# Two layers of a hybrid decoder: causal masks as matrix products, small S5 operations on GpSimd, six early input units instead of four

## The chip, the cores and the metric

One core of a Trainium2 chip runs the kernel. The metric is device microseconds of one execution. All times below are microseconds (us) unless they are marked ns. The engines are TensorE (PE, its weight loads PEld), VectorE (DVE), ScalarE (ACT), GpSimd (POOL) and SyncE (SP, which here only issues transfers).

## What is computed

One step of a decoder of two layers, for a prompt of 256 tokens and 8 samples with one new token each. The model has 1024 columns. Each layer computes (the reference, cut):

```python
h = x @ p['w_in']                      # 1024 x 2560
u_a, q_b, k_b, v_b, q_c, k_c, v_c, g_c = jnp.split(h, ...)
ya, s5r, s5i = s5_branch(u_a, ...)     # complex diagonal state space model
yb = sb_attend(q_b, k_b, v_b, bias, ...)          # 4 heads of 64
yc, ret_s = retention_branch(q_c, k_c, v_c, g_c, ...)
x = layer_norm(ALPHA * x + concat(ya, yb, yc) @ p['w_out'])
f, conv_new = conv_ffn(x, conv_prev, w_up, conv_w, conv_b, w_down)
x = layer_norm(ALPHA * x + f)
```

and in stick_breaking, where the mask is:

```python
z = q @ k * DH ** -0.5 + bias
valid = k_pos[None, :] < q_pos[:, None]
log_beta = jax.nn.log_sigmoid(z)
log_rest = jnp.where(valid, log_beta - z, 0.0)
tail = lax.cumsum(log_rest, axis=3, reverse=True) - log_rest
w = jnp.where(valid, jnp.exp(log_beta + tail), 0.0)
```

The S5 branch has 16 groups of 64 complex states. The prompt's states come from a scan over 256 steps; a sample's new state is a * x0 + f * (B u), and the prompt's last state is scaled by f too. All data are f32.

## The kernel before

**Data.** x lies transposed, 128 partitions x 8 blocks x 264 columns (256 prompt, 8 samples). The weights of a layer are cut into 94 units of 8 blocks of 128x128 (512 KB), which SP loads into a ring of 5 slots: 20 input units, 8 of w_out, 44 up, 22 down. One unit gives one tile of 128 output columns.

**Two ways to multiply.** Of the input units, 0 to 2 are taken raw ahead of the layer norm, and the others are f32 products, eight a unit (`tile8`, L432). An f32 product leaves two records in the trace. Nearly all units behind the inputs, and the units in EARLY, are split: weight and x become a high half (fp32r, rounded) and the low rest, and the product is hi x hi, hi x lo and lo x hi in one pass each (L439 to L441; L451 to L453 for the early ones). EARLY[1] is 16 to 19 before. For an early unit ScalarE writes we_hi (`split_hi_early`, L972), VectorE subtracts it from the ring's slot in place (`split_lo_early`, L1586), and x is split once, by ScalarE's `upper_early` (L978, xe_hi) and VectorE's two `lower_early` (L1593, xe_lo, four blocks of x each). TensorE waits for a unit's low half before its first product. An early unit's slot in the ring is used like any other.

**Order.** The order on each engine is written out by hand; the engines meet only through semaphores (`need` waits for a count, `claim` waits until a PSUM bank is read out). A table says behind which input unit each side step stands. In layer 0: the scores of the attention (sc) behind unit 7, S5's inputs of the first half (`s5_b`, b00, b01) at 2 and 3, of the second half (b10, b11) at 9 and 11, S5's readout c0 at 11 and c1 at 17, the tails at 16. In layer 1: scores behind 5, b10 at 6, b11 and c0 at 7, tails and c1 at 12, the gated products (glu, L581), retention (L633) and key transposes at 14.

**Attention.** q and k are rows of hb, a head has 64 of the 128 partitions: heads 0 and 2 the lower, 1 and 3 the upper half. `causal` gives each head's scores in two products (L622: 256 columns, L623: the second 128x128 block), `sb_scores` calls it for the four heads. ScalarE evacuates them to ZT (Z in the code, L1145) and makes softplus; VectorE multiplies the diagonal 128x128 blocks by a 0/1 mask (`sb_second`, L1877 and L1878), TensorE sums the tails (`sb_tails`, L744 to L751), VectorE subtracts (`sb_third`, L1884 to L1889), ScalarE takes exp, and VectorE multiplies by the mask again (`sb_mask`, L1894 and L1895).

**S5.** `s5_b` gives the inputs (L554, four products of 32 rows side by side), ScalarE copies them to BR and BI (`s5_evac`, L1139), VectorE scans (L1746, L1747), turns back (`s5_post`, L1781 to L1787) and takes the last states sfin (L1789, L1790). cf (L1665 to L1671) are the readout's coefficients. `s5_c` is the readout: 16 records for the prompt (L566), 16 for the samples (L571), which come from VectorE's small operations `s5_states` (six of 128x32, L1719 to L1725) and `s5_samples` (eight of 128x32, L1756 to L1765) for each half. `s5_finals` (six of 128x8, L1769 to L1775) makes the prompt's last states. `s5_skip` (L1968) adds D u to the readout.

**ScalarE in layer 0** also makes the tables of S5's turns (`turns_up`, L1091 to L1093). L1251 (zs) copies the samples' scores behind the main ones' place.

## Time and profile before

| | before |
|---|---|
| median of 3 runs | 674.18 |
| lowest, highest | 674.04, 674.87 |
| profiled execution | 674.94 |
| its span | 673.1 |
| TensorE busy | 661.4 (98%) |
| VectorE busy | 569.1 (85%) |
| ScalarE busy | 415.2 (62%) |
| GpSimd busy | 91.2 (14%) |
| TensorE's granted clock | full in all of the 40 slices |

The span goes from the first to the last instruction; the profiled execution's own time is 1.84 us longer. Engines work at the same time, so their busy times don't add up to the span. An engine does its instructions in order: one that waits holds all behind it.

### The profile page before, as it was taken

How to read it: one execution, taken by the hardware profiler on the slowest of the kernel's cores; microseconds unless marked ns; L12 is line 12 of the kernel's file. 1: busy time of each engine (PE TensorE's matmuls, PEld its weight loads, DVE VectorE, ACT ScalarE, POOL GpSimd, SP SyncE). 2: the span in 40 equal slices, each digit the busy share in tenths (PEclk: the TensorE clock that was granted, in tenths of full speed). 3: DMA queues.
4: the chain of work that ended last, by engine and by line, in shares of the span. 5: the costliest groups of instructions: out<-in, count | busy, mean ns of one | idle time of the engine just before them, and what ended most of it. 6: DMA issues, size and time to landing. Idle time of an engine off the chain costs nothing. (4 is left out here: it accounts for less than half of the span.)

```text
span 673.1 us, 13390 instructions
## 1 busy us (share of the span) xinstructions
PE 661.4 (98%) x5024; PEld 613.4 (91%) x5024; DVE 569.1 (85%) x1195; ACT 415.2 (62%) x690; POOL 91.2 (14%) x90
## 2 busy tenths in 40 slices
PE   8999999999999999999999999999999999999997
PEld 6777887989999999999987787989999999999996
DVE  5999999989998988789588998898999898884653
ACT  5776348758676666655847536786867666663343
POOL 0000010150222222200200000106012222220001
PEclk9999999999999999999999999999999999999999
DMA  8777540746674655664456463354765556555411
GB/s 315 244 274 220 188 130 6 274 112 227 203 255 151 201 187 184 197 192 142 142 179 228 167 206 125 115 200 167 199 211 197 188 170 193 176 196 190 161 57 66
DMA packets 42915, 121.82 MB, mean 181 GB/s; under 512 B 5538, under 2 KB 15170, under 8 KB 42338
## 3 DMA queue, kind: packets, MB, share of 16 engines
q1 hardware_dynamic: 40466, 115.22, 51.7%
q0 software_dynamic: 1088, 4.11, 2.5%
q10 hardware_dynamic: 1296, 1.63, 0.8%
q8 instruction: 40, 0.66, 0.4%
q14 instruction: 25, 0.20, 0.1%
HBM read 115.33 MB, written 5.61 MB: 180 GB/s over the span
## 5 line engine op out<-in xcount | busy, mean ns | idle before, releaser
L1579 DVE TENSOR_TENSOR w_lo<-ring,w_hi 128x1024 fp32r<-128x1024 f32 x144 | 175.4, 1220 | 30.6 <-ACT w_hi L964 29.0
L439 PE MATMUL ps<-x_hi,w_hi 128*128 128x264 f32 x672 | 191.0, 284 | 1.0 <-DVE x_lo L1529 1.0
L440 PE MATMUL ps<-x_lo,w_hi 128*128 128x264 f32 x672 | 190.4, 283 | 0.0
L441 PE MATMUL ps<-x_hi,w_lo 128*128 128x264 f32 x672 | 190.3, 283 | 0.0
L964 ACT CAST w_hi<-ring 128x1024 fp32r<-128x1024 f32 x144 | 150.2, 1043 | 59.4 <-PE ps L441 58.7
L439 PEld LDWEIGHTS ps<-x_hi,w_hi 128*128 128x128 f32 x672 | 126.5, 188 | 1.9 <-issue 1.8
L440 PEld LDWEIGHTS ps<-x_lo,w_hi 128*128 128x128 f32 x672 | 126.6, 188 | 0.0
L441 PEld LDWEIGHTS ps<-x_hi,w_lo 128*128 128x128 f32 x672 | 126.0, 188 | 0.0
L432 PE MATMUL ps<-x,ring 128*128 128x264 f32 x480 | 112.1, 390 | 0.1
L432 PEld LDWEIGHTS ps<-x,ring 128*128 128x128 f32 x480 | 89.1, 190 | 18.9 <-issue 2.2
L439 PE MATMUL ps<-hff_hi,w_hi 128*128 128x264 f32 x352 | 100.0, 284 | 0.0
L441 PE MATMUL ps<-hff_hi,w_lo 128*128 128x264 f32 x352 | 99.9, 284 | 0.0
L440 PE MATMUL ps<-hff_lo,w_hi 128*128 128x264 f32 x352 | 99.9, 284 | 0.0
L2190 POOL TENSOR_TENSOR hff_lo<-conv,hff_hi 128x264 fp32r<-128x264 f32 x44 | 52.7, 1198 | 213.8 <-ACT hff_hi L1208 213.8
L441 PEld LDWEIGHTS ps<-hff_hi,w_lo 128*128 128x128 f32 x352 | 66.3, 188 | 0.0
L439 PEld LDWEIGHTS ps<-hff_hi,w_hi 128*128 128x128 f32 x352 | 66.1, 188 | 0.0
L440 PEld LDWEIGHTS ps<-hff_lo,w_hi 128*128 128x128 f32 x352 | 66.1, 188 | 0.0
L1365 ACT ACTIVATE conv<-ps,vec 128x264 f32<-128x264 f32 x84 | 47.8, 569 | 22.2 <-PE ps L441 22.1
L1208 ACT CAST hff_hi<-conv 128x264 fp32r<-128x264 f32 x44 | 18.2, 414 | 48.8 <-DVE conv L1600 48.8
L2117 DVE SCALAR_TENSOR_TENSOR conv<-ps,vec,conv 128x254 f32<-128x254 f32 x84 | 40.5, 482 | 3.0
L1223 ACT COPY hb<-ps 128x264 f32<-128x264 f32 x34 | 12.7, 374 | 46.0 <-PE ps L432 43.5
L503 PE MATMUL ps<-zg,ring 128*128 128x266 f32 x160 | 39.0, 388 | 1.6 <-DMA ring<-in_units 1.6
(364 smaller groups left out, 1091.0 us busy)
## 6 DMA issues: line engine op xcount, KB each, us to landing
ring<-in_units SPq DMA_DIRECT2D x187, 512.0 KB, 3.5
kv<-in_kpool SPq DMA_DIRECT2D x32, 128.0 KB, 2.4
kv<-in_vpool SPq DMA_DIRECT2D x32, 128.0 KB, 2.4
SR<-in_sret SPq DMA_DIRECT2D x2, 1024.0 KB, 5.9
out_rsample<-SR POOLq DMA_DIRECT2D x2, 1024.0 KB, 5.1
out_kv<-hb ACTq DMA_DIRECT2D x2, 528.0 KB, 4.4
VBC<-v_rows POOLq DMA_DIRECT2D x8, 128.0 KB, 3.5
out_y<-x SPq DMA_DIRECT2D x3, 264.0 KB, 2.1
```

Of the source, the lines that this page charges most:

```text
L432: ins = mm(out, ring[:, ring_slot(n), k], rhs(k), start=(k == 0), stop=(k == 7))
L439: mm(out, wh, hi, start=start, stop=False)
L440: mm(out, wh, lo, start=False, stop=False)
L441: return mm(out, wl, hi, start=False, stop=stop)
L503: ins = mm(out[:, 0:GB], ring[:, ring_slot(raw_unit(q, i)), k], zgs[q % 2][:, k], start=(k == 0), stop=(k == KT - 1))
L964: E.did(nc.scalar.copy(w_hi[:, split_slot(i)], ring[:, ring_slot(n)]), "w_hi")
L1208: E.did(nc.scalar.copy(hff_hi[:, p], conv[:, (2 * p + 1) % CSLOTS]), "hff_hi")
L1223: E.did(nc.scalar.copy(hb[:, i], ps[:, in_bank(i), 0:T]), "in_evac")
L1365: E.did(f(conv[:, i % CSLOTS], source, ACT.Identity, scale=pv(L, "cw2", i), bias=pv(L, "cb", i)), "fc")
L1579: E.did(tt(w_lo[:, slot], ring[:, ring_slot(L * UNITS + i)], w_hi[:, slot].bitcast(F32), ALU.subtract), "w_lo")
L2117: E.did(stt(c[:, 2:SEQ], bank[:, 0:SEQ - 2], pv(L, "cw0", i), c[:, 2:SEQ], ALU.mult, ALU.add), "up_free")
L2190: E.did(tt(hff_lo[:, p], conv[:, (2 * p + 1) % CSLOTS], hff_hi[:, p].bitcast(F32), ALU.subtract), "hff_lo")
```

## The change

1. EARLY[1] is 14 to 19. The six we_hi share four homes in work and turn; units 18 and 19 wait until their home is free. In layer 1 ScalarE casts unit 14 behind upper_early, unit 15 behind the copy of tile 13, and 16 to 19 at glu. VectorE does both lower_early and the low half of 14 ahead of rotary, and the low half of 15 behind it.
2. The constant mask (0 or 1) becomes unseen (0 or -2^30). Two fp32r copies, of the identity and of unseen, are made by ScalarE in layer 0 behind unit 7's work. `causal` has a third product for each head, one-pass, 128 rows, 256 columns, which adds unseen to both diagonal blocks in PSUM. `sb_scores` waits for the two copies. VectorE's four mask products of a layer are gone.
3. s5_states, s5_samples and s5_finals are done by GpSimd, in its order ahead of its first transfer of each layer. It waits for x0, cf, the copies of the inputs, and the last states. New waits for its count: TensorE ahead of the samples' readout (L571), ScalarE ahead of the copy of the second half's inputs, SP ahead of the next layer's parameters.

```diff
-EARLY = [[], [16, 17, 18, 19]]
+EARLY = [[], [14, 15, 16, 17, 18, 19]]
...
-                 for e, (home, plane) in enumerate((("work", 0), ("work", 1), ("turn", 0), ("work", 3)))]
+                 for e, (home, plane) in enumerate((("work", 0), ("work", 1), ("turn", 0), ("work", 2), ("work", 0), ("work", 3)))]
...
-                mm(bank[:, 0:SEQ], kk[:, 0:P], qq[:, 0:SEQ], start=True, stop=True)
-                return mm(bank[:, SEQ:DEC], kk[:, P:SEQ], qq[:, P:SEQ], start=True, stop=True)
+                mm(bank[:, 0:SEQ], kk[:, 0:P], qq[:, 0:SEQ], start=True, stop=False)
+                mm(bank[:, SEQ:DEC], kk[:, P:SEQ], qq[:, P:SEQ], start=False, stop=False)
+                diagonal = bank.rearrange("p (a c) -> p a c", a=2)[:, :, 0:P]
+                return mm(diagonal, ident_r[:], bcast(unseen_r[:], [P, 2, P], 1), start=False, stop=True)
...
             def sb_scores(L):
                 needr(pe, "rawh", 2 * L, RAW)
+                pe.wait_ge(S("unseen"), 2)
...
                 for c in range(2):
                     for jj in range(HJ):
                         mm(bank[32 * jj:32 * jj + 32, 0:SEQ], cf[:, c, hf * HJ + jj], X[:, jj, 0:SEQ], ...)
+                pe.wait_ge(S("samples"), samples_done(L, hf))
...
-                need(act, "s5rd", L, 2)
-                need(act, "qk", L, 1)
+                need(act, "s5y", L, 2)
+                if i == EARLY[L][4]:
+                    tile_done(act, L, EARLY[L][0])
+                if i == EARLY[L][5]:
+                    need(act, "qk", L, 1)
...
                 if hf == 1 and c == 0:
                     need(act, "s5rd", L, 1)
+                    act.wait_ge(S("samples"), samples_done(L, 0))
...
                     if i == at_["sc"]:
+                        if L == 0:
+                            act.wait_ge(S("ld_cst"), 16)
+                            E.did(nc.scalar.copy(ident_r[:], C["ident"]), "unseen")
+                            E.did(nc.scalar.copy(unseen_r[:], C["unseen"]), "unseen")
                         need(act, "zst", L, 1)
...
-                E.did(stt(SPL[:], Z[:], 0.0, SPL[:], ALU.max, ALU.add))
-                E.settle()
-                d0, d1 = diagonals(SPL)
-                E.did(tt(d0, d0, mask, ALU.mult))
-                E.did(tt(d1, d1, mask, ALU.mult), "spl")
+                E.did(stt(SPL[:], Z[:], 0.0, SPL[:], ALU.max, ALU.add), "spl")
...
             @block.gpsimd
...
             for L in range(DEPTH):
+                for hf in range(2):
+                    s5_states(L, hf)
+                    E.settle()
+                    s5_samples(L, hf)
+                    E.settle()
                 if L == 0:
                     v_rows_back(L)
+                s5_finals(L)
                 need(pool, "s5st", L, 1)
```

How the order on the engines moves. TensorE, layer 0, the scores behind unit 7 (zsb are the samples' scores, hb holds q and k). Before:

```order
L735 MATMUL ps<-cst_130,zsb_58 128x128 x2
L622 MATMUL ps<-hb_49 128x256
L623 MATMUL ps<-hb_49 128x128
L622 MATMUL ps<-hb_49 128x256
L623 MATMUL ps<-hb_49 128x128
```

After:

```order
L748 MATMUL ps<-cst_134,zsb_58 128x128 x2
L632 MATMUL ps<-hb_49 128x256
L633 MATMUL ps<-hb_49 128x128
L635 MATMUL ps<-unseen_r_122,ident_r_121 128x2x128
L632 MATMUL ps<-hb_49 128x256
L633 MATMUL ps<-hb_49 128x128
L635 MATMUL ps<-unseen_r_122,ident_r_121 128x2x128
```

A product of 128 rows now stands between one head's two products and the next head's.

ScalarE at the same place, from the last set of S5's tables on (ZT takes the scores). Before:

```order
L1091 ACTIVATE tab1_84<-steps_133,fhi_98 128x256
L1092 ACTIVATE tab1_84<-steps_133,rnd_139,fhi_98 128x256
L1093 ACTIVATE low_85<-steps_133,flo_99 128x256
L1251 COPY ZT_54<-ps 128x64
L1145 ACTIVATE ZT_54<-ps,vec_129 128x384 x4
```

After:

```order
L1107 ACTIVATE tab1_86<-steps_137,fhi_100 128x256
L1108 ACTIVATE tab1_86<-steps_137,rnd_143,fhi_100 128x256
L1109 ACTIVATE low_87<-steps_137,flo_101 128x256
L1271 CAST ident_r_121<-cst_134 128x128
L1272 CAST unseen_r_122<-cst_134 128x128
L1274 COPY ZT_54<-ps 128x64
L1162 ACTIVATE ZT_54<-ps,vec_133 128x384 x4
```

The two copies that TensorE's scores wait for stand behind tile 7's tables.

VectorE, layer 1, from the end of the tails on (yd is S5's readout, work and hb take the rotary). Before:

```order
L1889 TENSOR_SCALAR ZT_54<-ZT_54 128x1600
L1968 SCALAR_TENSOR_TENSOR yd_106<-hb_49,vec_129,ps 128x264
L1799 TENSOR_TENSOR work_50<-hb_49,rope_132 128x1056
L1801 TENSOR_TENSOR hb_49<-hb_49,rope_132 128x1056
L1804 TENSOR_TENSOR hb_49<-hb_49,work_50 128x2x264
```

After:

```order
L1860 TENSOR_SCALAR ZT_54<-ZT_54 128x1600
L1933 SCALAR_TENSOR_TENSOR yd_108<-hb_49,vec_133,ps 128x264
L1617 TENSOR_TENSOR xe_lo_68<-x_70,xe_hi_73 128x1056 x2
L1610 TENSOR_TENSOR ring_lo_74<-ring_69,we_hi0_75 128x1024
L1780 TENSOR_TENSOR work_50<-hb_49,rope_136 128x1056
```

Three subtractions for the early units now stand between S5's skip and rotary.

## Rows read from the trace of the kernel before

**Rows 1.** The page: busy us, share of the span, instructions

```profile
PE 661.4 (98%) x5024; PEld 613.4 (91%) x5024; DVE 569.1 (85%) x1195; ACT 415.2 (62%) x690; POOL 91.2 (14%) x90
```

**Rows 2.** Waits of TensorE: us in total, times, longest us

```profile
PE ps L566 <- DVE sfin L1790: 1.2, 2, 0.7
...
PE ps L622 <- ACT hb L1223: 0.4, 1, 0.4
PE ps L693 <- DVE Oh L1822: 0.2, 1, 0.2
```

**Rows 3.** Timeline, TensorE, layer 0: start, us, instruction, [idle before <-releaser]

```profile
26.80 0.73 PE L554 MATMUL ps<-hb,s5b 32*128 32x264 f32 x8
27.46 3.83 PE L432 MATMUL ps<-x,ring 128*128 128x264 f32 x16
31.21 0.73 PE L554 MATMUL ps<-hb,s5b 32*128 32x264 f32 x8
...
45.03 0.71 PE L622 MATMUL ps<-hb 64*128 64x256 f32 x4
...
46.64 3.83 PE L432 MATMUL ps<-x,ring 128*128 128x264 f32 x16
```

**Rows 4.** Timeline, ScalarE, layer 0, around the scores

```profile
44.92 0.38 ACT L1223 COPY hb<-ps 128x264 f32<-128x264 f32 x1 [2.30 <-PE ps L432]
...
46.49 0.20 ACT L1251 COPY ZT<-ps 128x64 f32<-128x64 f32 x1
```

**Rows 5.** Source line L1380, ScalarE's cast of this size: shortest/mean/longest ns

```profile
L1380 ACT CAST mean_r<-cst x1: 289/289/289, 282.1 to 282.1; 128x128 fp32r<-128x128 f32 x1
```

**Rows 6.** Timeline, TensorE, layer 0, S5's second inputs and first readout

```profile
62.72 0.73 PE L554 MATMUL ps<-hb,s5b 32*128 32x264 f32 x8 [0.28 <-ACT work L1139]
64.17 1.07 PE L566 MATMUL ps<-work,cf 128*32 128x256 f32 x16 [0.73 <-DVE sfin L1790]
```

**Rows 7.** Timeline, TensorE, layer 1, the scores and what follows them

```profile
365.69 0.71 PE L622 MATMUL ps<-hb 64*128 64x256 f32 x4
...
367.91 0.49 PE L432 MATMUL ps<-x,ring 128*128 128x264 f32 x1
```

**Rows 8.** Timeline, TensorE, layer 1, units 8 to 16

```profile
381.95 14.41 PE L432 MATMUL ps<-x,ring 128*128 128x264 f32 x64
396.19 0.59 PE L744 MATMUL ps<-ZT,cst 128*128 128x256 f32 x2
396.62 0.38 PE L745 MATMUL ps<-ZT,cst 128*128 128x128 f32 x2
...
402.09 7.39 PE L432 MATMUL ps<-x,ring 128*128 128x264 f32 x32
409.31 1.94 PE L581 MATMUL ps<-yg,wglu 128*128 128x264 f32 x8
...
421.75 0.39 PE L451 MATMUL ps<-xe_hi,we_hi 128*128 128x264 f32 x1
...
424.76 1.04 PE L595 MATMUL ps<-cst,hb 128*128 128x128 f32 x8
```

**Rows 9.** Timeline, VectorE, layer 1: s5_skip, and the low half of unit 16

```profile
403.84 0.48 DVE L1968 SCALAR_TENSOR_TENSOR yd<-hb,vec,ps 128x264 f32<-128x264 f32 x1
...
416.79 1.22 DVE L1586 TENSOR_TENSOR ring_lo<-ring,we_hi 128x1024 fp32r<-128x1024 f32 x1
```

**Rows 10.** Windows, VectorE, samples: stretch, us, busy (operations), clock, DMA share, GB/s

```profile
48.75:49.95 1.20, 1.05 (x9) 1.00 0.13 40
```

**Rows 11.** GpSimd: a group by form (busy, mean ns), and one operation in the timeline

```profile
L2163 POOL TENSOR_TENSOR acc<-sqt 128x264 f32<-128x264 f32 x4 | 3.1, 773 | 110.2 <-ACT sqt L990 110.2
...
276.83 1.24 POOL L2190 TENSOR_TENSOR hff_lo<-conv,hff_hi 128x264 fp32r<-128x264 f32 x1 [4.57 <-ACT hff_hi L1208]
```

**Rows 12.** Timelines, layer 0: the last operation on cf (VectorE), the second inputs' copy (ScalarE)

```profile
56.37 0.42 DVE L1671 TENSOR_TENSOR cf<-cf,cft 128x256 f32<-128x256 f32 x1
...
61.54 1.04 ACT L1139 COPY work<-ps 128x1056 f32<-128x1056 f32 x1 [3.60 <-DVE work L1784]
```

More of the change, by code:

```diff
@@ L104 @@
 ROUND = 1.5 * 2.0**23
+SAMPLE_HALF = 6 + 8
+SAMPLE_STEPS = 2 * SAMPLE_HALF + 5
+UNSEEN = -2.0**30
 ROUND_15 = 1.5 * 2.0**8
@@ L202, in hybrid_step @@
         sqa = at("sqa", [P, 2, T], over=("acc", 0))
+        ident_r = at("ident_r", [P, P], dt=F32R)
+        unseen_r = at("unseen_r", [P, P], dt=F32R)
         eps_all, halfpi = at("eps_all", [P, 2]), at("halfpi", [P, 1])
@@ L753, in sb_values @@
             def sb_values(L):
-                need(pe, "w", L, 1)
+                need(pe, "wexp", L, 1)
                 need(pe, "vbt", L, 1)
@@ L768, in sb_sample_values @@
             def sb_sample_values(L):
-                need(pe, "w", L, 1)
+                need(pe, "wexp", L, 1)
                 pe.wait_ge(S("ld_kv"), 16 * NS * PAGES * (2 * L + 2))
@@ L1233, in _ @@
                                   "qb")
+                    if EARLY[L] and i == EARLY[L][0] - 1:
+                        split_hi_early(L, EARLY[L][1])
                     for hf in range(2):
@@ L1280, in _ @@
                             open_gates(L)
-                        for e in EARLY[L]:
+                        for e in EARLY[L][2:]:
                             split_hi_early(L, e)
@@ L1889, in sb_third @@
                 E.did(ts(Z[:], Z[:], 0.0, None, ALU.min), "zmin")
-            def sb_mask(L):
-                need(dve, "wexp", L, 1)
-                d0, d1 = diagonals(Z)
-                E.did(tt(d0, d0, mask, ALU.mult))
-                E.did(tt(d1, d1, mask, ALU.mult), "w")
             def sb_out(L):
@@ L2026, in _ @@
                 s5_skip(L, 1)
-                rotary(L)
-                sb_mask(L)
                 if EARLY[L]:
                     lower_early(L, 0)
+                    lower_early(L, 1)
+                    split_lo_early(L, EARLY[L][0])
+                rotary(L)
+                if EARLY[L]:
+                    split_lo_early(L, EARLY[L][1])
                 ret_inner(L)
@@ L2033, in _ @@
                 s5_out(L)
-                s5_finals(L)
                 if EARLY[L]:
-                    split_lo_early(L, EARLY[L][0])
+                    split_lo_early(L, EARLY[L][2])
                 sb_out(L)
-                if EARLY[L]:
-                    lower_early(L, 1)
                 conv_prev(L)
-                for e in EARLY[L][1:]:
+                for e in EARLY[L][3:]:
                     split_lo_early(L, e)
@@ L2154, in _ @@
         def _(pool):
-            E = Engine(pool, "pool_step")
+            E = Engine(pool, "samples")
             tt = nc.gpsimd.tensor_tensor
@@ L2164, in ln_squares, with s5_states, s5_samples, s5_finals @@
                           "lnacc2" if t == KT - 2 else "pool_ln")
+            def s5_states(L, hf):
+                if hf == 0:
+                    pool.wait_ge(S("ld_x0"), 16 * (L + 1))
+                    need(pool, "cf", L, 1)
+                jr = slice(hf * HJ, (hf + 1) * HJ)
+                ar, ai = bcast(are[:, jr], [P, HJ, NS], 2), bcast(aim[:, jr], [P, HJ, NS], 2)
+                x0r, x0i = s5x0[:, 0, jr], s5x0[:, 1, jr]
+                E.did(tt(stmp[:, 0], ar, x0r, ALU.mult))
+                E.did(tt(stmp[:, 1], ai, x0i, ALU.mult))
+                E.did(tt(stmp[:, 2], ar, x0i, ALU.mult))
+                E.did(tt(stmp[:, 3], ai, x0r, ALU.mult))
+                E.settle()
+                E.did(tt(stmp[:, 0], stmp[:, 0], stmp[:, 1], ALU.subtract))
+                E.did(tt(stmp[:, 2], stmp[:, 2], stmp[:, 3], ALU.add))
+            def s5_samples(L, hf):
+                jr = slice(hf * HJ, (hf + 1) * HJ)
+                fr, fi = (bcast(v[:, jr], [P, HJ, NS], 2) for v in (fre, fim))
+                need(pool, "buev", L, 2 * hf + 2)
+                br, bi = BR[:, :, SEQ:T], BI[:, :, SEQ:T]
+                if L > 0 and hf == 0:
+                    pool.wait_ge(S("st_s5"), 16 * L)
+                E.did(tt(smul[:, 0], fr, br, ALU.mult))
+                E.did(tt(smul[:, 1], fi, bi, ALU.mult))
+                E.did(tt(smul[:, 2], fr, bi, ALU.mult))
+                E.did(tt(smul[:, 3], fi, br, ALU.mult))
+                E.settle()
+                E.did(tt(smul[:, 0], smul[:, 0], smul[:, 1], ALU.subtract))
+                E.did(tt(smul[:, 2], smul[:, 2], smul[:, 3], ALU.add))
+                E.settle()
+                E.did(tt(s5o[:, 0, jr, 1:NS + 1], stmp[:, 0], smul[:, 0], ALU.add))
+                E.did(tt(s5o[:, 1, jr, 1:NS + 1], stmp[:, 2], smul[:, 2], ALU.add))
+            def s5_finals(L):
+                need(pool, "s5x", L, 2)
+                E.did(tt(lmul[:, 0], fre[:], sfin[:, 0], ALU.mult))
+                E.did(tt(lmul[:, 1], fim[:], sfin[:, 1], ALU.mult))
+                E.did(tt(lmul[:, 2], fre[:], sfin[:, 1], ALU.mult))
+                E.did(tt(lmul[:, 3], fim[:], sfin[:, 0], ALU.mult))
+                E.settle()
+                E.did(tt(s5o[:, 0, :, 0], lmul[:, 0], lmul[:, 1], ALU.subtract))
+                E.did(tt(s5o[:, 1, :, 0], lmul[:, 2], lmul[:, 3], ALU.add), "s5st")
             def v_rows_back(L):
@@ L2206, in constants @@
     cst = np.stack([np.full((P, P), 1 / P, f), np.full((P, P), 1 / D_MODEL, f), eye, (k >= q).astype(f),
-                    np.ones((P, P), f), (k < q).astype(f), np.full((P, P), 1 / 256, f),
+                    np.ones((P, P), f), np.where(k < q, 0, UNSEEN).astype(f), np.full((P, P), 1 / 256, f),
                     np.full((P, P), -1 / D_MODEL, f)], 1)
```

57 lines of the change are left out of this document (8 added, 49 removed).

## Prediction, made before the changed kernel was run

> **What bounds the kernel now.** I read the busy shares of the engines first: TensorE works for 661.4 us of a span of 673.1 [rows 1], so only two kinds of thing can move the time: work that TensorE gains or loses, and the 11.7 us in which it is idle. Next, TensorE's waits, one row for each releaser [rows 2]. Three of them touch this change: S5's readout, which waits for the last prompt states from VectorE (1.2 us in two places), the scores of layer 1 (0.4), and the retention of the samples (0.2). Then the timelines of TensorE and of the engine it follows, around each place that the change touches [rows 3 to 9]. A difference of starts in them is the time that a stage takes; the busy time of a group runs past the start of the next one, so I never add it. Every f32 product leaves two records: x64 is 32 products, four units.
>
> **Sizes.** Four f32 units took 381.95 to 396.19 [rows 8], 3.56 us each, or 0.445 for one product of 264 columns. An f32 product of 256 columns over the full height took 0.43 (396.19 to 396.62). A unit as 24 one-pass products took 421.75 to 424.76, 3.01 us, so 0.125 for a product, and 0.12 for the 256 columns of a mask.
>
> **Masks, layer 0: a wait for ScalarE.** Before, the scores start at 45.03 [rows 3]. Now they need both copies (ident_r, unseen_r). ScalarE does them in its order behind the copy of tile 7 (44.92) and the three L1091 to L1093 activations, where before it began its next work at 46.49 [rows 4]. Nothing there lets it begin earlier, since tile 7 comes from TensorE just before. A cast of 128x128 took 0.289 us [rows 5], two take 0.58: ready at 47.07. TensorE is in order, so everything behind waits too: **+2.04 us**. Nothing covers it.
>
> **Masks, both layers: the products themselves.** The eight score products of layer 0 took 45.03 to 46.64, 1.61 us [rows 3]. At 0.43 and half of that for 128 columns, four heads in a row would need 4 x 0.645 = 2.58. They took less because heads 0 and 1 stand in different halves of the array's rows (partitions 0 to 63 and 64 to 127) and two heads run together: 2 x 0.645 = 1.29, and 0.3 of something else. Now a mask product of all 128 rows stands behind each head. The next head's products, 64 rows, can't be loaded beside it, and the pairs fall apart: +1.29. The four masks are +0.49. The trace also has a price for going over between shapes. Eight records of L554 (four products side by side, 32 rows each, 264 columns) should take 0.445 and took 26.80 to 27.46, 0.66; the unit behind took 27.46 to 31.21, 3.75, where 3.56 is usual [rows 3]. So a change to narrower rows and one back cost about 0.2 each. Before there were two of them in the stage; now there are eight, +1.20. Sum **+2.98 us**: the stage goes from 1.61 to 4.59. The bounds are +0.49, if the masks only join the pairs, and +2.98; the 1.20 is the least certain, since the next weights may come in under the running product, and without it the sum is +1.78. I take 2.98, since the rows with a change of height show its price.
>
> In layer 1 the same stage took 365.69 to 367.91, 2.22 us with 0.4 of waiting for q and k of heads 2 and 3 [rows 7, 2]. Heads 0 and 1 now take so long that this wait is over by then. 4.59 - 2.22 = **+2.37**. The casts are from layer 0 and cost nothing here.
>
> The Trainium skill (TensorE: Matmul & The Clock Gate, "Step-by-step: what each phase is for") says that a weight load is pulled ahead of running products if its row groups don't conflict or if it goes to the background buffer. By the first half a mask's load must wait, by the second none need; by the second the 1.20 would be nothing, which is the second rival below. The rows on L554 speak against it.
>
> **What layer 0 gets back.** TensorE comes 5.02 us later to all that follows. It waited there 0.28 for the copy of S5's inputs and 0.73 for the prompt's last states [rows 6]. Neither hangs on the scores (VectorE's post-processing of the first half runs on from the scans), and VectorE is also rid of the samples' eight small operations, 1.20 us [rows 10]. Both waits go: **-1.01**. VectorE's six last small operations (s5_finals) go too, so the 0.2 behind Oh [rows 2] goes: **-0.20**. What comes next there is not late. Layer 0: 2.04 + 2.98 - 1.01 - 0.20 = **+3.81**.
>
> **S5 on GpSimd.** The rows for GpSimd's own speed are of 128x264: 0.773 us undisturbed, 1.24 where VectorE ran at the same time [rows 11]. The 128x32 operations lie between nothing and 0.773. On VectorE eight took 1.20 [rows 10], 0.15 each; I take about 0.2 for GpSimd. It is the latest in layer 0. The copy of the second half's inputs (61.54, 1.04 us) now waits for 14 operations of GpSimd, six states and eight samples, and these wait for cf, written at 56.37 + 0.42, 1.2 earlier now, so 55.6 [rows 12]. TensorE wants the copy's result at 62.44 + 5.02 = 67.46, so the copy must begin by 66.4: 10.8 us for 14 operations, 0.77 each, what eight times the columns cost. For the whole stretch to 62.7 VectorE runs two-input operations of 1.22 us (L1781 to L1787), then it waits for that same copy. The samples' products of S5's readout, which now wait for the same operations, come later still. In layer 1 cf is there long before, and GpSimd has more room. GpSimd's own transfers stand behind these operations now, but the first of them (VBC<-v_rows) waited for ScalarE's rows of v until long after; SP's loads of layer 1's parameters, which now wait for the same count, waited for layer 0's gated products anyway. So the move costs nothing on the path: **0**, with 0 below and the third rival above.
>
> The Trainium skill (SBUF — State Buffer, "Terms") says that VectorE and GpSimd share a port pair that one of them holds for a whole instruction, while the other blocks. The 1.24 against 0.773 agrees. By that rule one GpSimd operation would get in behind each 1.22 us operation, some seven until 62.7, and the last seven run alone by about 64.2: in time as well.
>
> **Six early units, layer 1.** The wait for the last states, 1.2 less the 0.73 of layer 0, goes, since TensorE comes 2.37 later: **-0.50**. Units 13 and 14 as f32 took 402.09 to 409.31, 7.22 us [rows 8]. Unit 14 is now split, and its low half is made by VectorE behind s5_skip, which can't start before S5's readout is done, and two lower_early. VectorE needs 0.48 (L1968) [rows 9], two subtractions of 1056 columns, by the 1.22 of 1024 columns [rows 9] 1.26 each, and 1.22: 4.22 us from the end of the readout. Unit 13 covers 3.56 of them. TensorE waits 0.66, then needs 3.01: 7.23, so unit 14's **gain is eaten: 0**. If ScalarE's casts for it came after that it would be more; they stand behind upper_early, which ended before the readout did. Unit 15 took half of 7.22, 3.61, and takes 3.01: **-0.60**; its low half is made during unit 14 and the gated products (L581, from 409.31). Units 16 to 19 are as before. VectorE's masks (four of 128x512 in a layer) also go; TensorE waits for none of these. Rotary now stands behind three subtractions, 3.7 us more, but its readers (L633, behind L581) come later too. Layer 1: 2.37 - 0.50 + 0 - 0.60 = **+1.27** (1.28 with the 0.01).
>
> **Sum.** 3.81 + 1.28 = +5.09. The profiled execution's own time is 674.94 (span 673.1 and 1.84 around it): 680.03. It was 0.76 above the median of the runs, 674.18; less that, **679.3**.
>
> **Rivals.** Forecast A: 679.3.
> B, the changes of height are hidden: each layer loses 1.20 less. 5.09 - 2.40 = 2.69, so **676.9**. For it: 0.3 of excess over 1.29 before is less than two times 0.2. Against it: L554, twice.
> C, GpSimd is late. If one small operation needs 1.0 us, by its own overhead or because VectorE shuts it out, 14 end at 69.6, the copy at 70.6, and TensorE waits 3.2 in layer 0: **682.5**. It decides from 0.77 us on. For it: no row shows so small an operation there, and 1.24 was seen. Against it: 0.773 for eight times the columns.
> D, not slower: the mask products run beside the heads' pairs as a third matmul at their own price. Layer 0 then grows by 0.49 beside the wait, 2.04 + 0.49 - 1.21 = 1.32; in layer 1 half of the masks fills the 0.4 of waiting, and the stage grows by 0.25, less 1.09 of gains (0.50 + 0.60 - 0.01) is -0.84. Sum +0.48: **674.7**. The place is the score stage alone: with both growths together under 1.6 us the change is no slower than the measurement tells. For it: the pairs did overlap in two halves. Against it: a product of 128 rows takes both halves.
>
> **How the numbers follow.** A has 0.57, B 0.20, C 0.10, D 0.10, and 0.03 is for D without the wait for ScalarE (2.04 less, 672.7). About 0.2% (1.35 us) is what a measurement of this kernel can tell from no change. A, B and C are slower by more: 0.87. D is within: 0.10. Faster: 0.03. The range goes from 676.2, 0.7 under B, to 682.6, so that it holds A, B and C, with 0.7 for the sizes of the casts and of the masks.
>
> **What would show it.** A gap of some 2 us on TensorE ahead of layer 0's first score product, released by ScalarE's second cast (right), or none. Score stages of some 4.6 us in both layers: 3.4 would be B, 2.1 D. S5's first readout without a wait in either layer, and layer 0's copy of S5's inputs released by TensorE or VectorE, not by GpSimd; if by GpSimd, C. A wait of 0.7 us ahead of unit 14, on the low half of its weights; if it is over 1.3, unit 14 is a loss. GpSimd's operations of 128x32 near 0.2 us. I would be wrong altogether if the two-halves pairing isn't what made the score stage short, or if the casts ran earlier.

## The result, and the profile after

| | before | after |
|---|---|---|
| median | 674.30 (4 runs) | 684.71 (4 runs) |
| lowest, highest | 674.04, 674.87 | 683.84, 685.92 |
| profiled execution, its span | 674.94, 673.1 | 684.63, 682.8 |
| mean granted clock of TensorE | 1.000 | 0.993 (the four runs: 0.988 to 0.993) |

The ratio is 1.0154, 95% interval 1.0137 to 1.0172. The change costs 10.4 us. The direction was forecast, the size was not: 679.3 with a range to 682.6. In the sets of runs beside the experiments, one run of the kernel before was a slow one (937.45, granted clock 0.656), and it is left out.

The page of the changed kernel answers to [rows 1], with the row of TensorE's granted clock in 40 slices (tenths of full speed):

```profile
PE 669.7 (98%) x5048; PEld 619.9 (91%) x5048; DVE 560.9 (82%) x1121; ACT 418.2 (61%) x694; POOL 132.1 (19%) x158
...
PEclk9997999999999999999999999999999999999999
```

TensorE has 8.3 us more of busy time. The fourth slice, about 51 to 68 us, has a granted clock of 0.7. No slice was so before. A 9 in this row means 90% or more, so a slice of 17 us can hide a loss of 1.7 us; the mean of a run is the finer sign (1.000 before). TensorE's waits (us in total, times, longest), which answer to [rows 2]:

```profile
PE ps L632 <- issue: 2.0, 1, 2.0
...
PE ps L460 <- issue: 0.4, 1, 0.4
PE ps L563 <- ACT work L1156: 0.3, 1, 0.3
```

The wait ahead of the scores (L632) is there, and a small one ahead of unit 14 (L460). The view names no releaser for the first, but ScalarE's second cast ended at 47.43 and the scores began at 47.54. The waits for S5's last states and for Oh are gone. L563 is S5's second inputs, in layer 1; in layer 0 it has no wait. Timeline of TensorE in layer 0, the answer to [rows 3]:

```profile
45.18 0.38 PE L748 MATMUL ps<-cst,zsb 128*128 128x128 f32 x2
47.54 0.67 PE L632 MATMUL ps<-hb 64*128 64x256 f32 x2 [1.98 <-issue]
48.05 0.38 PE L633 MATMUL ps<-hb 64*128 64x128 f32 x2
48.36 0.40 PE L635 MATMUL ps<-unseen_r,ident_r 128*128 128x256 f32 x1
48.68 1.22 PE L632 MATMUL ps<-hb 64*128 64x256 f32 x2
...
54.81 5.72 PE L441 MATMUL ps<-x,ring 128*128 128x264 f32 x16
60.36 0.60 PE L718 MATMUL ps<-cst,hb 128*128 128x128 f32 x4
```

and in layer 1, the answer to [rows 7] and [rows 8]:

```profile
374.43 0.70 PE L632 MATMUL ps<-hb 64*128 64x256 f32 x2
...
378.98 3.72 PE L441 MATMUL ps<-x,ring 128*128 128x264 f32 x16
...
412.46 3.83 PE L441 MATMUL ps<-x,ring 128*128 128x264 f32 x16
...
419.67 1.94 PE L591 MATMUL ps<-yg,wglu 128*128 128x264 f32 x8
```

The same stage takes 4.55 us in layer 1 (374.43 to 378.98) and 7.27 in layer 0 (47.54 to 54.81). Before, the unit behind the stage began at 46.64 [rows 3] and what follows it at 50.30:

```profile
50.30 0.60 PE L706 MATMUL ps<-cst,hb 128*128 128x128 f32 x4
```

The windows of these stretches (us, busy time of PE, PEld, DVE, ACT and POOL, granted clock, DMA share, GB/s) tell why:

```profile
45.50:47.54 2.04, 0.07 (x2) 0.03 (x1) 2.04 (x5) 2.04 (x7) 0.00 (x0) 1.00 0.51 126
47.54:48.68 1.14, 1.14 (x5) 0.82 (x5) 1.14 (x4) 0.01 (x1) 0.00 (x0) 0.96 0.96 386
48.68:54.80 6.12, 6.12 (x16) 4.45 (x16) 5.81 (x9) 1.74 (x3) 0.00 (x0) 0.50 0.09 33
54.80:57.00 2.20, 2.20 (x6) 1.69 (x6) 2.13 (x5) 1.92 (x2) 0.65 (x1) 0.50 0.00 0
374.43:378.98 4.55, 4.55 (x22) 3.46 (x21) 4.52 (x7) 3.01 (x6) 2.65 (x5) 1.00 0.40 119
```

About 1.1 us behind the wait the granted clock fell to 0.50, which is 1.2 instead of 2.4 GHz, and a head took 2.09 us (48.68 to 50.77) where it takes 1.16 in layer 1. The clock stayed there through the stage and into the next unit. That is 7.27 - 4.55 = 2.72 in the stage and 5.55 against 3.66 for the unit behind it (54.81 to 60.36, before 46.64 to 50.30), 1.89 more: **4.61 us of half clock**. In e1, which has the same order at full clock, this unit took 3.56, by which it would be 4.7.

### The profile page after: what moved, and what is told of

It reads as the page before. It is cut to its first block, busy times and chain, and to the rows that moved or that the text cites. A ratio compares the mean times of both kernels' runs of the same rounds, so it can differ in the third digit from the quotient of the medians.

```text
span 682.8 us, 13448 instructions
## 1 busy us (share of the span) xinstructions
PE 669.7 (98%) x5048; PEld 619.9 (91%) x5048; DVE 560.9 (82%) x1121; ACT 418.2 (61%) x694; POOL 132.1 (19%) x158
## 4 chain that ended last, share of the span: by engine, by line
PE 91%; DVE 5%; issue 1%; ACT 1%; DMA 1%; SPq 0%; DVEq 0%; ACTq 0%
PE ps L448 20%; PE ps L449 20%; PE ps L450 20%; PE ps L441 15%; PE ps L512 2%; DVE z L1507 1%; DVE z L1515 1%; PE ps L632 1%; DMA ring<-in_units 1%; PE ps L460 1%; PE ps L461 1%; PE ps L462 1%; PE ps L563 1%; PE ps L575 1%; PE ps L739 1%
## 5 line engine op out<-in xcount | busy, mean ns | idle before, releaser
L441 PE MATMUL ps<-x,ring 128*128 128x264 f32 x448 | 106.5, 395 | 0.3 <-ACT x L1053 0.3
L441 PEld LDWEIGHTS ps<-x,ring 128*128 128x128 f32 x448 | 84.8, 193 | 18.3 <-issue 2.2
L450 PEld LDWEIGHTS ps<-hff_hi,w_lo 128*128 128x128 f32 x352 | 66.4, 189 | 0.0
```

The costliest lines, as they stand in the source:

```text
L441: ins = mm(out, ring[:, ring_slot(n), k], rhs(k), start=(k == 0), stop=(k == 7))
L450: return mm(out, wl, hi, start=False, stop=stop)
```

## The experiments

The runs differ in how long TensorE's clock was at half, so one number is worked out for each of them. While the clock is at half, each microsecond does half a microsecond's work, so a run loses (1 - mean granted clock) x span. For the changed kernel that is 4.8, 8.2, 6.1 and 6.1 us, and without it the four runs would have taken 679.9, 677.7, 677.7 and 678.6. The profiled one agrees: 4.8 by this, 4.6 or 4.7 by the trace. The clock has three digits, which is 0.3 us either way, and e3's two runs at 1.000 are no faster than its four at 0.996 or 0.997, so I trust it to 1 or 2 us. I call it the time at full clock. Each ratio is against the runs of the kernel before that were taken beside it; their medians are 674.28 to 674.43.

| kernel | median | ratio, 95% interval | granted clock of its runs | time at full clock |
|---|---|---|---|---|
| after | 684.71 | 1.0154 (1.0137 to 1.0172) | 0.988 to 0.993 | 677.7 to 679.9 |
| e1 early copies | 679.67 | 1.0071 (1.0050 to 1.0092) | 0.993 to 0.998 | 675.1 to 676.8 |
| e2 only the wait | 676.05 | 1.0029 (1.0016 to 1.0041) | 0.997 in 3 of 6, else 1.000 | 674.5 to 675.6 |
| e3 masks last | 676.57 | 1.0032 (1.0020 to 1.0045) | 0.996 or 0.997 in 4 of 6, else 1.000 | 674.0 to 677.0 |
| e4 both | 678.59 | 1.0066 (1.0049 to 1.0083) | 0.994 to 0.997 | 675.0 to 675.9 |
| e5 e4, S5 on VectorE | 673.66 | 0.9991 (0.9982 to 1.0000) | 0.998 to 1.000 | |
| e6 only S5 on GpSimd | 678.37 | 1.0056 (1.0042 to 1.0070) | 0.996, 0.997 | |
| e7 only six early units | 676.48 | 1.0031 (1.0020 to 1.0042) | 0.997 to 1.000 | |
| e8 only masks, e4's form | 674.04 | 0.9993 (0.9984 to 1.0002) | 0.998 to 1.000 | |
| e9 wait filled | 681.24 | 1.0091 (1.0073 to 1.0109) | 0.994 to 0.996, one 1.000 | 677.7 to 679.0 |
| e11 e4, states early | 672.79 | 0.9977 (0.9968 to 0.9986) | 0.998 to 1.000 | |
| e12 after, S5 on VectorE | 684.39 | 1.0149 (1.0125 to 1.0173) | 0.989 to 0.995 | 678.4 to 679.0 |
| e13 e11, pairs broken | 678.82 | 1.0067 (1.0044 to 1.0091) | 0.992 to 0.997, two 1.000 | 675.7 to 677.6 |

**What makes the clock fall: the wait or the broken pairs?** Before, the products of two heads, in different halves of the array's rows, stood side by side and overlapped: a pair. In the changed kernel a mask product of the full height stands between them: the pairs are broken. e1 takes the wait away, e2 has the wait alone, e3 keeps the wait and has its pairs back, e4 has neither fault.

e1, on the changed kernel:

```diff
@@ ScalarE, unit sc
-                            E.did(nc.scalar.copy(ident_r[:], C["ident"]), "unseen")
-                            E.did(nc.scalar.copy(unseen_r[:], C["unseen"]), "unseen")
@@ ScalarE, unit ss (one earlier), layer 0
+                            E.did(nc.scalar.copy(ident_r[:], C["ident"]), "unseen")
+                            E.did(nc.scalar.copy(unseen_r[:], C["unseen"]), "unseen")
```

> The changed kernel with one edit: ScalarE makes the two fp32r copies for the masks behind unit 6, where it was idle for 2.3 us, instead of behind unit 7. Theory 1 (the wait of 1.98 us ahead of layer 0's scores made TensorE's clock fall from full to half, and the half clock cost some 4.6 us more): wait and half clock both go, 684.7 - 2.0 - 4.6 = 678.1, granted clock 1.00 throughout. Theory 2 (the score stage itself, with its broken pairs, made the clock fall): only the wait goes, 682.7, clock still 0.50 in layer 0's stage.

679.67. The wait went, and layer 0's stage ran at full clock (44.53 to 49.09, 4.56 us). But three of the four runs still lose clock (0.993 to 0.996; the fourth has 0.998, which the kernel before has too), and the profiled one shows a dip in layer 1, at the end of the same stage, with no wait ahead of it (timeline, TensorE):

```profile
370.14 0.70 PE L632 MATMUL ps<-hb 64*128 64x256 f32 x2
370.67 0.38 PE L633 MATMUL ps<-hb 64*128 64x128 f32 x2
370.98 0.38 PE L635 MATMUL ps<-unseen_r,ident_r 128*128 128x256 f32 x1
371.30 0.78 PE L632 MATMUL ps<-hb 64*128 64x256 f32 x2
371.88 0.63 PE L633 MATMUL ps<-hb 64*128 64x128 f32 x2
...
372.81 4.90 PE L441 MATMUL ps<-x,ring 128*128 128x264 f32 x16
```

L633 goes from 0.38 to 0.63, and the unit behind takes 4.90. Theory 2 had the clock fall without the wait, but in layer 0; theory 1 had no fall left. A new wait also came up in layer 0, 1.07 us for the copy of S5's second inputs; it is followed below.

e2, on the kernel before:

```diff
+                            E.did(nc.scalar.copy(wait_a[:], C["ident"]), "eps_set")
+                            E.did(nc.scalar.copy(wait_b[:], C["mask"]), "eps_set")
...
             def sb_scores(L):
                 needr(pe, "rawh", 2 * L, RAW)
+                pe.wait_ge(S("eps_set"), 8)
```

> The kernel before with the wait alone: ScalarE makes two casts of 128x128 at the place of the changed kernel's, into tiles that nobody reads, and TensorE waits for them ahead of layer 0's scores. No mask products, S5 and early units as before. Theory 1 (the wait makes the clock fall): 2.0 for the wait, up to 4.6 for the half clock in the 9 us behind it, 1.0 of later waits taken up: 674.3 + 5.6 = 679.9. Theory 2 (the stage with broken pairs does it): the clock stays full, 674.3 + 2.0 - 1.0 = 675.3.

676.05, between the two. The wait of 1.98 us is there; three runs kept a full clock (675.0 to 675.6, what theory 2 says), three lost 0.003 of it, 2 us. The profiled run is one that kept its clock, so where the others lost it no trace of e2 shows; e3's does.

e3, on the changed kernel:

```diff
                 for h in range(HEADS):
                     need(pe, "in_evac", L, KB + 1 + h // 2 - RAW)
-                    bank = claim(4 + h, "zev", L, h + 1)
-                    E.did(causal(bank, h, KB, QB_), "sbz")
+                    banks.append(claim(4 + h, "zev", L, h + 1))
+                    causal(banks[h], h, KB, QB_)
+                for h in range(HEADS):
+                    E.did(hide(banks[h]), "sbz")
```

> The changed kernel with another order of the scores: the eight products of the four heads first, in pairs as before, then the four mask products. Casts and wait as in the changed kernel. If the broken pairs are the cost, layer 1's stage goes from 4.55 to some 2.4 us and layer 0's too at full clock, 2.2 less in each. Theory 1 (the wait makes the clock fall): the clock is still half behind the wait, 684.7 - 4.4 = 680.3 or a little less. Theory 2 (the broken pairs make it fall): 684.7 - 4.4 - 4.6 = 675.7. If pairs don't matter: no change from 684.7.

676.57, 8.1 us less than the changed kernel from the order of twelve products. Layer 1's stage has its pairs back (timeline, TensorE):

```profile
367.60 0.71 PE L632 MATMUL ps<-hb 64*128 64x256 f32 x4
368.13 0.39 PE L633 MATMUL ps<-hb 64*128 64x128 f32 x4
368.90 0.78 PE L632 MATMUL ps<-hb 64*128 64x256 f32 x4 [0.38 <-ACT hb L1246]
369.44 0.46 PE L633 MATMUL ps<-hb 64*128 64x128 f32 x4
369.83 0.75 PE L638 MATMUL ps<-unseen_r,ident_r 128*128 128x256 f32 x4
370.42 3.73 PE L441 MATMUL ps<-x,ring 128*128 128x264 f32 x16
```

2.82 us with the wait of 0.38, where the changed kernel has 4.55; layer 0's would be 2.2 at full clock (e4: 44.57 to 46.76). So the broken pairs cost 2.4 and 1.7 in the two layers, 4.1 together (I had written 4.4); the other 4 of the 8.1 are clock that came back: four runs still lose 0.003 or 0.004 of it, two nothing. Where the profiled one lost it stands in its windows of 40 to 60 us (the clock is behind the five busy times), first before, then the changed kernel, then e3:

```profile
40.00:60.00 20.00, 20.00 (x124) 16.05 (x113) 19.48 (x33) 12.21 (x23) 0.00 (x0) 1.00 0.76 265
40.00:60.00 20.00, 18.02 (x85) 13.34 (x78) 19.55 (x26) 9.10 (x20) 3.65 (x4) 0.74 0.38 148
40.00:60.00 20.00, 18.02 (x98) 14.78 (x91) 19.52 (x26) 11.88 (x23) 4.87 (x5) 0.91 0.63 234
```

and, in e3, in the score products behind the wait, with the pairs whole (timeline, TensorE):

```profile
46.25 0.81 PE L632 MATMUL ps<-hb 64*128 64x256 f32 x4 [1.98 <-issue]
...
47.28 1.06 PE L632 MATMUL ps<-hb 64*128 64x256 f32 x3
...
48.69 1.22 PE L638 MATMUL ps<-unseen_r,ident_r 128*128 128x256 f32 x4
```

The four mask products take 1.22 here and 0.75 in layer 1, and the score products at 47.28 are slow already, ahead of any mask. So a wait of 2 us can make the clock fall with whole pairs, but not in every run, and for less long than in the changed kernel.

e4 has both edits, e1's and e3's.

> Both edits: copies behind unit 6, and the masks behind all eight products. By theory 1 and the pairs: 684.7 - 2.0 - 4.6 - 4.4 = 673.7, about as before the change; some 0.5 more if the waits of 1.2 us for S5's last states, which the lateness had covered, come back in part.

678.59, slower than e3, and 5 above what was expected. The stages are right (44.57 to 46.76 in layer 0), but TensorE now waits elsewhere (TensorE's waits), and behind the wait of 3.46 us in layer 0 its clock fell (L581 took 0.42 at 67.50, where it takes 0.29); all four runs lost some:

```profile
PE ps L563 <- ACT work L1162: 3.8, 2, 3.5
```

**The filled wait.** e9 leaves the changed kernel as it is and gives TensorE work in the wait:

```diff
+                first = claim(4, "zev", L, 1)
+                if L == 0:
+                    for _ in range(4):
+                        mm(first[:, 0:T], C["ident"], x[:, 0], start=True, stop=True)
                 pe.wait_ge(S("unseen"), 2)
```

> The changed kernel, with four more f32 products of the full height (1.8 us) that TensorE does into head 0's bank ahead of layer 0's wait for the mask copies; their result is overwritten by the scores. Nothing else moves, the scores start at the same time. If TensorE's idle time ahead of the stage makes the clock fall: the wait shrinks to some 0.2 us, the clock stays full, 684.7 - 6 = 679. If the stage of the broken pairs does it alone: 684 with a granted clock of 0.99 as before. If both add up: between, some 681, as in e1_early_casts, where the dip came in layer 1 instead.

681.24, the case in which both add up. The scores start as long behind the samples' scores as in the changed kernel (2.31 us, there 2.36), so the filler itself saves no time: at full clock these runs give 677.7 to 679.0, as the changed kernel's do. By this number the 3.5 us are clock alone. The clock still fell in four of five runs, in the profiled one later in the stage (L632 took 0.70 at 49.19 and 1.22 at 50.54). The fifth kept it and took 678.55: it does all that the changed kernel does, and is the run that comes nearest to what the sum of the prediction is about. What TensorE did before the fall differs: before, 1.98 us of nothing and 1.1 us of the stage; here 3.2 us of the stage alone.

e13 has broken pairs, no wait, and nothing late on GpSimd; it is e11 (below) with this undone:

```diff
-                for h in range(HEADS):
-                    E.did(hide(banks[h]), "sbz")
...
+                    E.did(causal(bank, h, KB, QB_), "sbz")
```

> The kernel of e11_states_early with one edit undone: each head's mask product stands behind that head's scores again, so the pairs are broken; no wait ahead of the stage, GpSimd in time. By the prediction's price (4.59 for a stage against 2.2 with the masks last): 672.8 + 2.4 in layer 0 + 2.1 in layer 1 - 0.3 of waits taken up = 677.0 in a run whose clock stays full. If the broken pairs alone also make the clock fall: 1 to 4 more in most runs, 679 as a median, with a granted clock of 0.993 to 0.998. If the clock needs the wait too: 677.0 and a clock of 0.999 or 1.000.

678.82. Two of seven runs kept the clock, 676.83 and 677.57, where 677.0 was written; the others took 1 to 5.5 us more (678.37 to 682.61). In the profiled one the clock fell in the last head of layer 0's stage (timeline, TensorE; the lines of the sources stand two lower, L634 and L635 are L632 and L633 of the changed kernel, L637 its L635):

```profile
48.06 0.38 PE L637 MATMUL ps<-unseen_r,ident_r 128*128 128x256 f32 x1
48.38 0.83 PE L634 MATMUL ps<-hb 64*128 64x256 f32 x2
49.00 0.63 PE L635 MATMUL ps<-hb 64*128 64x128 f32 x2
49.56 0.58 PE L637 MATMUL ps<-unseen_r,ident_r 128*128 128x256 f32 x1
49.94 4.86 PE L443 MATMUL ps<-x,ring 128*128 128x264 f32 x16
```

| what TensorE's stage has | runs | of them with a granted clock under 0.998 |
|---|---|---|
| wait of 2 us and broken pairs (after, e12) | 9 | 9 (0.988 to 0.995) |
| broken pairs, no wait (e13) | 7 | 5 |
| wait of 2 us, whole pairs (e2, e3) | 12 | 7 (0.996, 0.997) |
| whole pairs, no wait (e5, e8, e11) | 33 | 0 |

Broken pairs with the 2 us of idle time gone or filled lose clock too in e1 (three of four runs) and e9 (four of five). Longer waits elsewhere, with whole pairs, do the same: 3.5 us in e4 (four of four runs) and 3.9 in e6 (five of five), both below; a wait of 2.0 us ahead of unit 14 does it in four of e7's eight runs. Nor is the fall unknown to the kernel before: beside the experiments one of its 61 runs (677.31, in e13's set) had 0.996. Why the same program keeps its clock in one run and not in another no run here shows.

**GpSimd.** The wait in e4 is the prediction's rival C. Its GpSimd timeline:

```profile
55.42 1.21 POOL L2140 TENSOR_TENSOR stmp<-are,s5x 128x32 f32<-128x32 f32 x1 [54.15 <-DVE cf L1701]
56.59 1.22 POOL L2141 TENSOR_TENSOR stmp<-aim,s5x 128x32 f32<-128x32 f32 x1
...
61.40 1.23 POOL L2146 TENSOR_TENSOR stmp<-stmp 128x32 f32<-128x32 f32 x1
62.71 0.24 POOL L2156 TENSOR_TENSOR smul<-fre,work 128x32 f32<-128x32 f32 x1
...
64.37 0.25 POOL L2165 TENSOR_TENSOR s5o<-stmp,smul 128x32 f32<-128x32 f32 x1
```

An operation of 128x32 takes 0.24 us alone and 1.22 while VectorE runs its two-input operations of 1.22. By the Trainium skill (SBUF — State Buffer, "Terms") VectorE and GpSimd share a port pair that one holds for a whole instruction, while the other blocks. The order agrees, one GpSimd operation for each of VectorE's. That VectorE is blocked for as long as GpSimd's operation lasts alone, 0.24 us, does not show: its operations start some 1.18 us apart here, and 1.14 in the kernel before. The copy can start at 64.6; TensorE wanted its result at 62.4 and got it at 65.9. In the changed kernel itself the same copy is released by GpSimd too, and TensorE, 10 us late, didn't notice (timelines, GpSimd's last operation and TensorE):

```profile
65.29 0.25 POOL L2159 TENSOR_TENSOR s5o<-stmp,smul 128x32 f32<-128x32 f32 x1
...
72.43 0.73 PE L563 MATMUL ps<-hb,s5b 32*128 32x264 f32 x8
```

The copy stands between them, from 65.65 to 66.69. Without the 4.6 us of half clock TensorE would have been there at 67.8, still 1.1 us behind it.

e5 is e4 with all of part 3 undone:

```diff
@@ VectorE
+                s5_samples(L, 0)
...
@@ GpSimd
-                    s5_states(L, hf)
-                    s5_samples(L, hf)
...
@@ ScalarE, copy of the second half's inputs
-                    act.wait_ge(S("samples"), samples_done(L, 0))
```

> The kernel of e4_both with S5's small operations back on VectorE, at their places of the kernel before: copies behind unit 6, masks behind all eight products, six early units. Theory G (GpSimd's small operations take 1.21 us each beside VectorE's two-input ones, and hold up the copy of S5's second inputs as soon as TensorE is not 5 us late): the wait of 3.46 us in layer 0 goes and with it the dip of the clock behind it, 678.6 - 3.2 - 2 = 673.4. If GpSimd is not the cause of that wait: 678 as before.

673.66: the wait went, and the clock stayed at 0.998 or more in all eleven runs.

e6 is the kernel before with part 3 alone:

```diff
@@ VectorE
-                s5_samples(L, 0)
...
@@ GpSimd
+                    s5_states(L, hf)
+                    s5_samples(L, hf)
```

> The kernel before with the small S5 operations on GpSimd alone; masks on VectorE, four early units. Theory G: cf at 55.6, six states at 1.2 us each beside VectorE, eight samples alone at 0.24, so the copy of S5's second inputs starts at 65.0 instead of 61.5 and TensorE waits some 3.4 us there instead of 0.28; the 0.73 and 0.5 of later waits go: 674.3 + 3.1 - 1.4 = 676.0, and up to 2 more where the clock dips behind the wait. If GpSimd is in time (as the prediction had it): 674.3 - 1.2 = 673.1.

678.37, 4.0 slower than before, with part 3 alone on the kernel before. The wait is 3.93 us (expected 3.4), and the clock falls behind it (windows, the wait and then what follows):

```profile
62.38:66.32 3.94, 0.01 (x1) 0.03 (x1) 0.84 (x4) 1.18 (x2) 3.55 (x15) 1.00 0.60 211
66.32:69.55 3.23, 3.23 (x40) 1.61 (x41) 2.37 (x2) 3.17 (x4) 0.16 (x1) 0.50 0.76 227
```

e12 is the changed kernel with the same lines as in e5 undone, and its masks and copies as they are.

> The changed kernel with S5's small operations back on VectorE, all else as in the changed kernel (late copies, masks between the heads, six early units). The prediction's term for the move to GpSimd was 0, since TensorE is so late there: 684.7 within 1. If GpSimd costs something in the changed kernel too: 682 or less. Alone on the kernel before it cost 4.0 (e6_pool_only), so costs don't add up if this stays at 684.7.

684.39 against 684.71: in the changed kernel part 3 costs nothing that these runs can tell, as the prediction had it, though alone it costs 4.0. (The five runs lie 4.7 us apart; at full clock they give 678.4 to 679.0, the changed kernel's 677.7 to 679.9.) The costs of the parts don't add up, since one lateness covers the other.

e11 mends part 3 in place of taking it out. The states need only are and aim, which VectorE writes well ahead of cf:

```diff
@@ VectorE, s5_factor
                 E.did(tt(fim[:], t3, den, ALU.mult))
+                factor_at.append(E.last)
@@ GpSimd, s5_states
-                    need(pool, "cf", L, 1)
+                    pool.wait_ge(S(factor_at[L][0]), factor_at[L][1])
```

> The kernel of e4_both (copies early, masks last, S5's small operations on GpSimd, six early units), in which GpSimd's states wait only for the factors that they read, which VectorE has some 17 us before cf in layer 0. Theory G (one GpSimd operation for each of VectorE's): even at 1.2 us each the 14 operations end before 61.5, so TensorE's wait of 3.46 us for the copy of S5's second inputs goes, with the dip of the clock behind it: 678.6 - 3.2 - 2 = 673.4, the same as with the samples on VectorE (673.7) or 0.3 less. If GpSimd slows VectorE by as much as it takes: VectorE's scans of layer 0 come later by up to 0.5 us for each operation, and S5's readout waits: 675 and more.

**672.79, the fastest kernel of this study: 1.5 us under the kernel before (674.28 beside it) and 11.9 under the changed one.** GpSimd now begins at 34.95, where it began at 56.35 in the changed kernel (more than the 17 us that I had written), and is done with the first half's samples and the second half's states by 47.6, at 0.23 to 1.23 us each. The full clock stayed in all eleven runs within 0.002.

**The early units and the masks alone.**

e7 is the kernel before with part 1 alone, rotary and sb_mask behind the low half of unit 14:

```diff
-EARLY = [[], [16, 17, 18, 19]]
+EARLY = [[], [14, 15, 16, 17, 18, 19]]
...
                 s5_skip(L, 1)
+                if EARLY[L]:
+                    lower_early(L, 0)
+                    lower_early(L, 1)
+                    split_lo_early(L, EARLY[L][0])
                 rotary(L)
                 sb_mask(L)
                 if EARLY[L]:
-                    lower_early(L, 0)
+                    split_lo_early(L, EARLY[L][1])
```

> The kernel before with six early units alone. By the prediction's terms unit 14 brings 0 (a wait of 0.4 to 0.7 us for its low half) and unit 15 brings 0.6: 673.7. If moving rotary and the masks behind three subtractions makes the retention or the values late: slower, 674.5 or more, with a wait ahead of the retention's products in layer 1.

676.48, 2.1 slower, with part 1 alone on the kernel before. The wait is not ahead of the retention but ahead of unit 14 (timelines, TensorE and VectorE):

```profile
402.64 3.83 PE L432 MATMUL ps<-x,ring 128*128 128x264 f32 x16
408.46 0.36 PE L451 MATMUL ps<-xe_hi,we_hi 128*128 128x264 f32 x1 [1.99 <-DVE ring_lo L1592]
...
404.40 0.48 DVE L1974 SCALAR_TENSOR_TENSOR yd<-hb,vec,ps 128x264 f32<-128x264 f32 x1
```

S5's readout ended at 402.64, but VectorE was still at the tails' subtractions and came to s5_skip only at 404.40. In the changed kernel, where it has neither masks nor samples ahead of that, it was there 0.17 us behind the readout (412.63). The prediction's term for unit 14 holds only with VectorE relieved. Behind the wait the clock fell too: a one-pass product took 0.28, and 0.42 from 409.65 on.

e8 is the kernel before with part 2 alone, in the form of e4:

```diff
@@ VectorE
-                sb_mask(L)
...
@@ TensorE
+                for h in range(HEADS):
+                    E.did(hide(banks[h]), "sbz")
```

> The kernel before with the masks on TensorE alone, in the better form: copies behind unit 6, the four mask products behind the eight score products. The stages grow by 0.6 us (2.19 against 1.61 in layer 0 of e4_both) and by 0.3; the waits for S5's last states (0.73 and 0.5) go in part, since TensorE is later and VectorE has 1.3 us less to do ahead of them in layer 1: 674.3 + 0.9 - 1.2 = 674.0. If the clock dips on account of mask products even in this form: 675 and more, with a granted clock of 0.997.

674.04: the masks alone, in the good form, neither gain nor lose against 674.41 of the runs beside it. e5 is e8 with the six early units added: they bring 0.4 there, which is no more than the width of the two intervals can hide, and cost 2.1 in e7.

## Why the prediction was wrong, by its own steps

- **The wait for ScalarE.** +2.04 forecast; idle for 1.98, and 2.05 more of lateness (the list under "It adds up"), ready behind the two casts as worked out. Right.
- **The score stage.** 4.59 forecast, 4.55 measured in layer 1 and 4.56 in layer 0 of e1, where the clock was full. Layer 1 grew by 2.33 (378.98 - 374.43 less 2.22), forecast 2.37. Right as a sum, and rival B's 3.4 is out. How it splits into lost overlap (1.29), changes of height (1.20) and masks (0.49, measured 0.58 in e4) no run shows by itself. A head's three products start 0.53, 0.32 and 0.31 us apart (second head of layer 1 in the changed kernel) for sizes of 0.43, 0.22 and 0.12, so some 0.1 is lost also between two products of the same height. A price for changes of height alone is not the whole account. The half of the Trainium skill's sentence on weight loads (TensorE: Matmul & The Clock Gate, "Step-by-step: what each phase is for") by which none need wait is not borne out by this stage, if the weight loads are what costs the time; that no run takes apart.
- **What layer 0 gets back.** -1.01 and -0.20 forecast. TensorE was 10.06 us later than before at L718, 8.92 later behind the first readout and 8.74 later at layer 1's scores, so -1.14 and -0.18. Right.
- **S5 on GpSimd.** 0 forecast, 0.3 less with it on VectorE (e12), inside the spread. The price of one operation was taken as 0.2 and is 0.24 alone and 1.22 beside VectorE. The fourteen ended at 65.54, where the prediction gave them until 66.4: six were held to VectorE's pace and eight ran alone, where it had worked out seven and seven from the Trainium skill's rule. By the prediction's own sign (the copy released by GpSimd) this would be rival C, and it was not: TensorE wanted the result later still. Right for this kernel, but only under its lateness.
- **Six early units.** TensorE was 10.37 later at the start of unit 13 and 10.36 at its gated products, so unit 14 brought 0. Its start came 4.23 us behind the readout's end, forecast 4.22. (The view has 0.40 of waiting against 0.66 forecast, since it counts unit 13's time to the end of its last record.) From there to L605 (434.44, before 424.76 [rows 8]) it got 0.68 back, unit 15, forecast 0.60. The wait for the last states went, with 0.70 (11.07 to 10.37), forecast 0.50. Right, on one silent premise: that VectorE is at s5_skip when the readout ends. Before, it came 1.75 us behind it (403.84 against 402.09 [rows 8, 9]), and in e7 1.76; only parts 2 and 3 took that away.
- **It adds up.** 4.61 of half clock and the forecast 5.09 make 9.70. TensorE's lateness against before: 0.46 ahead of layer 0's samples' scores (the start, no part of the change), 2.51 at the scores, 8.17 behind them, 10.06 at L718, 8.92 behind the first readout, 8.74 at layer 1's scores, 11.07 behind them, 10.37 at unit 13, 9.68 at L605, and 9.7 at the end of the span.
- **The sum.** At full clock the four runs give 677.7 to 679.9, mean 678.5; the forecast was 679.3. e9's run at full clock took 678.55.

The step that failed stands nowhere in the sum: **it took TensorE's clock as full**. All the cost terms were worked out at the full clock of the kernel before, in which all 40 slices show it, and I never asked whether 2 us of idle time and a stage of half-height products, one behind the other, would leave it there. They don't: 4.6 us in the profiled execution (2.72 + 1.89), 4.8 to 8.2 in the four runs, mean 6.3. That 9.7 less 4.61 is just the forecast 5.09 is in part luck: 0.46 of it was there ahead of the change, and the waits that went and unit 15 gave back some 0.4 more than forecast. "What would show it" had the gap of 2 us right and 4.6 us for both stages, which is right in layer 1 only; for a longer stage, the 7.27 of layer 0, it had no meaning.

The row of the granted clock before (full in every slice) shows what TensorE got with no wait of 2 us and with whole pairs, and nothing of what it gets without. The fall of the clock should have been a rival of its own; with the largest loss of the four runs, 8.2, added to the sum the range would have reached 687.5.

## What to carry to other kernels

Products of half the array's height are cheap in pairs and expensive alone; put what needs the full height behind all of them, not between them. A stall of TensorE of some 2 us, or a stage in which products of part of its height stand singly, has to be costed twice, once as time and once as what the clock may do behind it, and the second can be the larger. A part moved to GpSimd should wait for just what it reads, and be given room of one VectorE operation for each of its own; a part that costs nothing under another part's delay must be measured without that delay.

## What the runs showed of the hardware

- The granted clock fell from 1.00 to 0.50 within one stage with TensorE "busy" all the time in the windows. It fell in all 9 runs with a wait of 2 us and broken pairs, in 5 of 7 with broken pairs alone, in 7 of 12 with the wait alone, and in none of 33 with neither (in one of 61 of the kernel before); the time of one and the same program ranged over 5.8 us (e13: 676.83 to 682.61).
- GpSimd's operations of 128x32 take 0.24 us alone and those of 128x8 about 0.2, so their time hardly depends on their size there; beside VectorE's two-input operations of 1.22 us they take 1.22. Beside VectorE's scans they took 0.52 to 0.63 (e11, 44.10 to 46.98). VectorE lost little by it: its six operations from 56.23 in the changed kernel took 1.23 to 1.28 each, before 1.22 or 1.23.
- Four f32 score products of 64 rows in two halves overlap; with a product of 128 rows between them the stage of four heads took 4.55 us, with the same four mask products behind them 2.19.
